# Transposes of the second phase made by DMA on SyncE's queue instead of TensorE, with the steps moved

## The reference, cut to what matters

```python
xn = rmsnorm(x, norm_attn_g)
q, k, v, gate_b, gate_c, h = split(xn @ w_in)      # three groups of 4 heads x 64; windows 128, 512, 2048, dilations 1, 4, 16
attn = heads' softmax attention per group, groups weighted by their softmax denominators
conv = gate_b * causal_conv3(gate_c * h)
x = x + concat(attn, conv) @ w_out
x = x + square(relu(rmsnorm(x, norm_mlp_g) @ w_up)) @ w_down
y = rmsnorm(x, norm_final_g)
```

## Time and profile before

| | us |
|---|---|
| median of 3 runs | 3246.47 (3242.42 to 3248.24) |
| the profiled execution, its own time | 3248.41 |
| its span, slowest core | 3246.7 |
| spans of the eight cores | 3194.0 to 3246.7 |
| TensorE busy in the span | 3035.3 (93%) |
| VectorE, ScalarE, GpSimd busy | 1334.1, 1080.6, 187.3 |

### The profile page before, as it was taken

The page is one execution under the profiler, slowest core; times in us unless marked ns, Lnnn a source line. Parts: engine busy times, 40 slices in busy tenths (PEclk is TensorE's granted clock), DMA queues, the critical chain, the costliest instruction groups (busy, mean ns, idle before and its releaser), DMA issues.

```text
span 3246.7 us, 65561 instructions; the slowest of 8 cores (3194.0 to 3246.7 us)
## 1 busy us (share of the span) xinstructions
PE 3035.3 (93%) x23299; PEld 1948.8 (60%) x23299; DVE 1334.1 (41%) x2927; ACT 1080.6 (33%) x2399; POOL 187.3 (6%) x232
## 2 busy tenths in 40 slices
PE   5997859899997799999999999999999999999998
PEld 2654435565554466666666666666666666666665
DVE  5355426637444234333343333333343333433332
ACT  4244225436334223222232323323232233323232
POOL 3101200101000000000000000000000000000000
PEclk9998979999998899999999999999999999999999
DMA  9124925536134825444254343543535425333130
GB/s 198 37 67 115 79 43 130 129 70 149 34 131 178 206 51 132 104 103 120 55 141 109 86 119 58 155 109 69 122 64 145 121 57 125 77 117 107 38 114 21
DMA packets 168411, 331.62 MB, mean 102 GB/s; under 512 B 31840, under 2 KB 124000, under 8 KB 165984
## 3 DMA queue, kind: packets, MB, share of 16 engines
q1 hardware_dynamic: 94080, 172.92, 16.5%
q0 software_dynamic: 70672, 67.19, 15.9%
q10 hardware_dynamic: 3344, 87.30, 9.2%
HBM read 309.57 MB, written 176.39 MB: 150 GB/s over the span
## 4 chain that ended last, share of the span: by engine, by line
PE 84%; DMA 4%; ACT 3%; issue 3%; DVE 3%; SPq 1%; another core or an unknown queue 1%; POOL 0%; ACTq 0%; DVEq 0%; POOLq 0%
PE pp L750 28%; PE pp L739 26%; PE pp L566 12%; PE pp L678 7%; PE pp L533 4%; DMA NZ<-osb 3%; ACT junkB L875 1%; PE pp L536 1%; PE pp L688 1%; DMA w_in_sb<-w_in 1%; PE pp L582 1%; SPq L1328 1%; PE pp L701 1%; PE pp L663 1%; PE pp L511 1%
## 5 line engine op out<-in xcount | busy, mean ns | idle before, releaser
L739 PE MATMUL pp<-xn1T,w_up_sb 128*128 128x256 bf16 (+1 forms) x8448 | 1071.2, 271 | 29.3 <-ACT hr L901 26.6
L750 PE MATMUL pp<-w_down_sb,h1T 128*128 128x512 bf16 x4160 | 1057.9, 379 | 17.9 <-DMA w_down_sb<-w_down_b 17.9
L739 PEld LDWEIGHTS pp<-xn1T,w_up_sb 128*128 128x128 bf16 x8448 | 804.1, 98 | 281.1 <-issue 39.3
L901 ACT ACTIVATE hr<-pp 128x256 bf16<-128x256 f32 (+1 forms) x1056 | 394.6, 380 | 1181.6 <-PE pp L739 1173.9
L1150 DVE TENSOR_TENSOR h1T<-hr 128x256 bf16<-128x256 bf16 (+1 forms) x1056 | 301.0, 289 | 1003.1 <-ACT hr L901 936.5
L750 PEld LDWEIGHTS pp<-w_down_sb,h1T 128*128 128x128 bf16 x4160 | 402.7, 98 | 299.6 <-issue 19.0
L566 PE MATMUL pp<-xnT,w_in_sb 128*128 128x512 bf16 x2304 | 536.6, 382 | 24.2 <-DMA w_in_sb<-w_in 8.8
L566 PEld LDWEIGHTS pp<-xnT,w_in_sb 128*128 128x128 bf16 x2304 | 212.0, 98 | 268.9 <-issue 37.2
L678 PE MATMUL pp<-w_out_sb,attnT 128*128 128x512 bf16 x1040 | 249.7, 384 | 9.0 <-DMA attnT<-cvT 9.0
L858 ACT ACTIVATE PT<-pp 128x1024 bf16<-128x1024 f32 x171 | 174.2, 1023 | 145.3 <-PE pp L586 143.8
L1022 DVE TENSOR_TENSOR PT<-PT,mask 128x1024 bf16<-128x1024 bf16 (+1 forms) x192 | 129.4, 674 | 198.8 <-ACT PT L858 185.3
(11 more groups left out here) (136 smaller groups left out, 1984.0 us busy)
## 6 DMA issues: line engine op xcount, KB each, us to landing
kvs<-ck ACTq DMA_DIRECT2D x16, 4080.0 KB, 21.2
xt<-xp SPq DMA_DIRECT2D x64, 512.0 KB, 5.3
xtB<-xp SPq DMA_DIRECT2D x64, 512.0 KB, 3.8
yp<-xtB SPq DMA_DIRECT2D x64, 512.0 KB, 3.1
NZ<-osb SPq DMA_DIRECT2D x192, 130.0 KB, 2.3
NZt<-NZ SPq DMA_DIRECT2D x64, 390.0 KB, 4.6
kvs<-ck ACTq DMA_DIRECT2D x16, 1008.0 KB, 6.4
sK<-ck POOLq DMA_DIRECT2D x52, 256.0 KB, 6.7
```

The source lines that it names most:

```text
L739: ins = e.matmul(bank(v % 2)[:, 0:N], lhsT=w_up_sb[:, i // 8, kc, (i % 8) * 128:(i % 8 + 1) * 128], rhs=xn1T[T % 2][:, kc, 0:N], start=kc ...
L750: ins = e.matmul(psD[s][:, half * 512:(half + 1) * 512], lhsT=h1T[v % NH][:, s * 128:(s + 1) * 128], rhs=w_down_sb[:, i, half * 512:(half ...
L901: e.activation(out=hr[v % NHR][:, 0:N], in_=bank(v % 2)[:, 0:N], func=AF.Relu).then_inc(s_hr, 1)
```

## The change

The steps b and sT, and the first half of d, leave TensorE; the copies after b (ScalarE) and sT (VectorE) go. In their place SyncE issues DMA transposes from SBUF to SBUF: b from attn_n to attnT, a new step t from xn1 to xn1T, and sT from sK to sKTc. What d keeps is VectorE's multiply by the gain, in place in xn1T. Who waited for TensorE's transposes now waits for these DMAs (a, n and d on VectorE, c and sS on TensorE, the load of sK on GpSimd's queue). The bank B_T is not used any more. In FIRST_B and SLOTS the steps stand elsewhere: b two slots earlier, in the slots of a; c in 13, 15, 17 and 19 (was 15, 17, 19, 21); n in 19 and 23 (was 21 and 25); t in 20 and 24; d in 26 and 30 (was 25 and 29); sT in 13 and 25 (was 17 and 31).

```diff
 FIRST_B = [(-1, "LX", 0, 0), (-1, "LX", 0, 1), (-1, "LN", 0, 0), (0, "LN", 0, 1), (0, "LC", 0, 0), (0, "a", 0, 0),
-           (2, "b", 0, 0), (2, "LN", 1, 0), (3, "a", 0, 1), (4, "c", 0, 0, 0), (5, "b", 0, 1), (5, "LN", 1, 1),
-           (6, "c", 0, 0, 1), (8, "c", 0, 1, 0), (9, "n", 0, 0), (10, "c", 0, 1, 1), (11, "d", 0, 0), (13, "n", 0, 1),
-           (14, "d", 0, 1)]
+           (1, "b", 0, 0), (2, "LN", 1, 0), (3, "a", 0, 1), (4, "b", 0, 1), (5, "c", 0, 0, 0), (5, "LN", 1, 1),
+           (6, "c", 0, 0, 1), (8, "c", 0, 1, 0), (9, "n", 0, 0), (9, "t", 0, 0), (10, "c", 0, 1, 1), (12, "d", 0, 0),
+           (13, "n", 0, 1), (13, "t", 0, 1), (15, "d", 0, 1)]
...
-        SLOTS = {1: [("sP", -1, 0), ("LC", 1), ("E", -1, 0)], 3: [("E", -1, 1)], 5: [("y", -1, 0), ("ST", -1, 0), ("LX", 1, 0), ("a", 1, 0)],
-                 7: [("y", -1, 1), ("ST", -1, 1), ("LX", 1, 1), ("b", 1, 0)], 9: [("a", 1, 1)], 11: [("b", 1, 1), ("LN", 2, 0)],
-                 13: [("LN", 2, 1)], 15: [("c", 1, 0, 0)], 17: [("c", 1, 0, 1), ("sT", -1, 1)], 19: [("c", 1, 1, 0)],
-                 21: [("n", 1, 0), ("c", 1, 1, 1)], 23: [("sS", -1, 1)], 25: [("d", 1, 0), ("n", 1, 1)], 26: [("sP", -1, 1)],
-                 29: [("d", 1, 1)], 31: [("sT", 0, 0)], 33: [("sS", 0, 0)]}
+
+        SLOTS = {1: [("sP", -1, 0), ("LC", 1), ("E", -1, 0)], 3: [("E", -1, 1)],
+                 5: [("y", -1, 0), ("ST", -1, 0), ("LX", 1, 0), ("a", 1, 0), ("b", 1, 0)],
+                 7: [("y", -1, 1), ("ST", -1, 1), ("LX", 1, 1)], 9: [("a", 1, 1), ("b", 1, 1)], 11: [("LN", 2, 0)],
+                 13: [("LN", 2, 1), ("c", 1, 0, 0), ("sT", -1, 1)], 15: [("c", 1, 0, 1)], 17: [("c", 1, 1, 0)],
+                 19: [("n", 1, 0), ("c", 1, 1, 1)], 20: [("t", 1, 0)], 23: [("sS", -1, 1), ("n", 1, 1)], 24: [("t", 1, 1)],
+                 25: [("sT", 0, 0)], 26: [("sP", -1, 1), ("d", 1, 0)], 30: [("d", 1, 1)], 33: [("sS", 0, 0)]}
...
         def b_bank(T):
 
-            return (0, 1) if T == 0 else (B_T, B_M)
+            return 1 if T == 0 else B_M
+
+        def tr_done(W, sems, q):
+
+            W.wait_ge(sems[q % 2], 16 * (q // 2 + 1))
...
             for kind, T, i, *half in events:
-                pst = bank_bf(b_bank(T)[0] if kind in "bd" else B_T).rearrange("p (k t) -> p k t", k=8)
-                if kind == "b":
+                if kind == "c":
                     q = nsubs_before(T) + i
+                    W.wait_ge(s_wo, 16)
                     if T == 0:
                         W.wait_ge(s_free["act"], P.nev["act"])
                         W.wait_ge(s_free["dve"], P.nev["dve"])
-                    W.wait_ge(s_an, q + 1)
-                    W.wait_ge(s_xn1T, nsubs_before(T))
-                    W.wait_ge(s_aTs, q)
-                    W.wait_ge(s_ktc, min(2 * T - 3, NBAT))
-                    for kc in range(6):
-                        ins = e.transpose(out=pst[:, kc, :], in_=attn_n[:, kc * 128:(kc + 1) * 128], identity=ident[:])
-                    ins.then_inc(s_aT, 1)
-                elif kind == "c":
-                    q = nsubs_before(T) + i
-                    W.wait_ge(s_wo, 16)
                     if T < 32:
-                        W.wait_ge(s_aTs, q + 1)
+                        tr_done(W, s_aT, q)
                     else:
                         W.wait_ge(s_sat, 1)
                     W.wait_ge(s_bcv[q % 2], 16 * (q // 2 + 1))
@@ -675,35 +670,13 @@
                         W.wait_ge(s_x1, m)
                     W.wait_ge(s_so, min(2 * T - 3, NBAT))
                     for kc in range(8):
-                        ins = e.matmul(bank(b_bank(T)[1]), lhsT=attnT[q % 2][:, kc, :],
+                        ins = e.matmul(bank(b_bank(T)), lhsT=attnT[q % 2][:, kc, :],
                                        rhs=w_out_sb[:, kc, half[0] * 512:(half[0] + 1) * 512], start=kc == 0, stop=kc == 7)
                     ins.then_inc(s_m, 1)
-                elif kind == "d":
-                    q = nsubs_before(T) + i
-                    W.wait_ge(s_xn1, q + 1)
-                    W.wait_ge(s_aTs, min(nsubs_before(T) + nsub(T), 64))
-                    W.wait_ge(s_ktc, min(2 * T - 2, NBAT))
-                    W.wait_ge(s_xn1T, q)
-                    for kc in range(8):
-                        ins = e.transpose(out=pst[:, kc, :], in_=xn1[:, kc * 128:(kc + 1) * 128], identity=ident[:])
-                    ins.then_inc(s_xT1, 1)
-                elif kind == "sT":
-
-                    b = T
-                    g, bb, t0, nq = BATCHES[b]
-                    W.wait_ge(s_ldk, 16 * (b + 1))
-                    if b % 2 == 0:
-                        W.wait_ge(s_xn1T, nsubs_before(b // 2 + 1) + nsub(b // 2 + 1))
-                    else:
-                        W.wait_ge(s_aTs, nsubs_before(b // 2 + 2) + 2)
-                    for u in range(4):
-                        for p in range(2):
-                            ins = e.transpose(out=pst[:, u * 2 + p, :], in_=sK[:, u, p * 128:(p + 1) * 128], identity=ident[:])
-                    ins.then_inc(s_kt, 1)
                 elif kind == "sS":
                     b = T
                     g, bb, t0, nq = BATCHES[b]
-                    W.wait_ge(s_ktc, b + 1)
+                    W.wait_ge(s_kt, 16 * (b + 1))
                     W.wait_ge(s_x1, done_x1(b // 2 + 1 + b % 2))
                     if b:
...
-                if kind == "b":
-                    q = nsubs_before(T) + i
-                    W.wait_ge(s_aT, q + 1)
-                    if q >= 2:
-                        W.wait_ge(s_m, 2 * (q - 1))
-                    e.activation(out=attnT[q % 2][:, 0:6, :], in_=pst[:, 0:6, :], func=AF.Copy).then_inc(s_aTs, 1)
-                elif kind == "c" and half[0] == 1:
+                if kind == "c" and half[0] == 1:
...
                 elif kind == "a":
                     q = nsubs_before(T) + i
                     if T:
-                        W.wait_ge(s_xT1, nsubs_before(T))
+                        tr_done(W, s_xT1, 2 * T - 2)
+                        tr_done(W, s_xT1, 2 * T - 1)
                     else:
                         phase_a_left(W)
                     nzv = NZt[q % 2][:].rearrange("p (g h e) -> p g h e", g=3, h=4)
                     W.wait_ge(s_bnz[q % 2], 16 * (q // 2 + 1))
                     if q:
-                        W.wait_ge(s_aT, q)
+                        tr_done(W, s_aT, q - 1)
...
-                elif kind == "sT":
-                    b = T
-                    W.wait_ge(s_kt, b + 1)
-                    if b:
-                        W.wait_ge(s_ss, b)
-                    e.tensor_copy(out=sKTc[:].rearrange("p u k t -> p (u k) t"), in_=pst).then_inc(s_ktc, 1)
...
                 elif kind == "n":
                     q = nsubs_before(T) + i
                     xrow = xtB[sl][:, i, :]
                     W.wait_ge(s_br, q + 1)
                     W.wait_ge(s_x1, 2 * q + 2)
-                    W.wait_ge(s_xT1, q)
+                    if q:
+                        tr_done(W, s_xT1, q - 1)
                     e.tensor_scalar(out=xn1[:], in0=xrow, scalar1=rsB[NORM["c", T, i] % 4], scalar2=None,
                                     op0=ALU.mult).then_inc(s_xn1, 1)
                 elif kind == "d":
                     q = nsubs_before(T) + i
-                    W.wait_ge(s_xT1, q + 1)
+                    xr = xn1T[sl][:, :, i * 128:(i + 1) * 128]
+                    tr_done(W, s_xT1, q)
                     W.wait_ge(s_ldgm, 16)
-                    if T >= 2:
-                        W.wait_ge(s_u, 32 * (T - 1))
-                    e.tensor_tensor(out=xn1T[sl][:, :, i * 128:(i + 1) * 128], in0=pst,
+                    e.tensor_tensor(out=xr, in0=xr,
                                     in1=g_mlp_sb[:, :].unsqueeze(2).broadcast_to([128, 8, 128]), op=ALU.mult
                                     ).then_inc(s_xn1T, 1)
                 elif kind == "up":
...
                 if b:
-                    W.wait_ge(s_kt, b)
+                    W.wait_ge(s_kt, 16 * b)
...
+                elif kind == "b":
+                    q = nsubs_before(T) + i
+                    W.wait_ge(s_an, q + 1)
+                    if q >= 2:
+                        W.wait_ge(s_m, 2 * (q - 1))
+                    e.dma_start_transpose(out=attnT[q % 2][:, 0:6, :], in_=attn_n).then_inc(s_aT[q % 2], 16)
+                elif kind == "t":
+                    q = nsubs_before(T) + i
+                    W.wait_ge(s_xn1, q + 1)
+                    if T >= 2:
+                        W.wait_ge(s_u, 32 * (T - 1))
+                    e.dma_start_transpose(out=xn1T[sl][:, :, i * 128:(i + 1) * 128], in_=xn1[:]).then_inc(s_xT1[q % 2], 16)
+                elif kind == "sT":
+                    b = T
+                    W.wait_ge(s_ldk, 16 * (b + 1))
+                    if b:
+                        W.wait_ge(s_ss, b)
+                    e.dma_start_transpose(out=sKTc[:].rearrange("p u k t -> p (u k) t"),
```

(22 more changed lines are left out.)

## The result

The changed kernel takes **3537.2 us** (median of 4 runs, 3516.0 to 3544.9) against 3246.6 us of the kernel before (4 runs, 3242.4 to 3248.2). The ratio is 1.088, its 95% interval 1.082 to 1.094. The change costs 291 us; the forecast was a gain of 62, and the result lies 227 us above the top of the range.

A forecast was written before the change was run, and what follows sets the result against it. TensorE, busy 93% of the span, was taken to bound the kernel. -72 us removed and +10 at the first phase's end made -62: 3248.4 to 3186.4 us profiled, median 1.9 lower, 3184.5; range 3168 to 3310.

The forecast's parts named there:

- What is removed, -72: TensorE's transposes of attention rows, cached keys and MLP rows: 74.5 us, less 2.3 ahead of the wait for w_down.
- ScalarE's squares at the tile's edge: Named as what TensorE waits for once per tile in the second phase: 26.6 us over 33 tiles.
- The landing, 4 us: Time for a DMA transpose on SP's queue to land, bounded from other DMAs; 2.5 to 3.5 us at plain pace.
- upper bound of 20 to 26 us: Transpose landing beside the cache copy: 64 KB took 6.0 us more there, and transposes have three or four times the rows.
- The deadlines: Time each second-phase transpose is allowed before its user waits, from 9.0 us for b(T+1,0); none missed at 4 us, cost 0.
- its cover: Slack between a second-phase transpose's issue and its user, first of all 9.0 us; 25 us for sT(T-1,1).
- The end of the first phase, +10: First attention-row transposes meet the weight loads: 3 to 7 us for the first, 2 to 5 for three others; bounds 0 to 25.
- sum of -62: Whole kernel: -72 for transposes removed and +10 at the first phase's end, giving 3184.5 us; forecast chance 0.52.
- Rival B: Even tiles: the cache copy slows some transposes, 16 tiles x 2.5 = +40 us, kernel at 3226; chance 0.12.
- Rival A: Transposes are long, so SP's queue or TensorE at c waits; 3284 us at 1.35 us per block; chance 0.29.
- r = 0.92: Time in us per 128x128 block from which b(T+1,0) passes its allowed 9.0 us at c in slot 13.
- 0.29 for slower: Chance that the whole kernel gets slower, all of it from long transposes; 0.12 of it below 3310 us.

The follow-up runs named there:

- run 3: Changed kernel with the same cache copies issued after up 28 instead of up 13, half the bytes in each tile; 3170.8 us, 0.980 of the kernel before.
- run 4: Kernel before the change, with its cache copies moved in the same way (after up 28, half in each tile); 3223.4 us, ratio 0.996.
- run 1: Changed kernel without the DRAM to DRAM copies of the caches; 3168.4 us, 0.979 of the kernel before.

## Why the prediction was wrong

- **What is removed, -72.** Nearly right. In runs 3 and 4 the second phase, first up to last up, takes 2082 to 2089 us against 2151 to 2152 (2080 to 2085 against 2150 to 2152 without the copy): core by core -63 to -71, on average -66 with the copy and -69 without. The few us that are missing fit the per-tile pace, 64.5 measured for 64.2. What the forecast calls ScalarE's squares at the tile's edge are its relus.
- **The landing, 4 us.** Right where no copy is in flight: medians of 3.2 to 4.7 in runs 1 and 3. The upper bound of 20 to 26 us was an error. It scaled the 6.0 us that 64 KB of attnT had lost beside the copy with the number of rows, and so held the copy at 22.1 us whatever stood beside it. It took 70.0, and landings went to 74.8.
- **The deadlines.** The list was right (9.0, 13, 25, 13 us), and all are met in tiles without a copy, but for 3 us at c beside the weight loads. In the copy's tiles sT, which had the longest allowance of all, is missed first, because it is issued within some 1.5 us of the copy. What I called its cover, slack of 25 us, was not enough to ask for; the question was what else is in flight when it is issued.
- **The end of the first phase, +10.** Right in kind, too small. The first up of run 3 comes at 1061.6 against 1041.3 in run 4 (+20, mean of eight cores), on the slowest core 1074.0 against 1052.5 (+21.5); inside my bounds of 0 to 25. b(0,0) landed after 20.0 us where I had added 3 to 7.
- **The forecast as a whole.** The sum of -62 is near what the change does without the meeting: -56 without the copy, -53 with it moved. That 3170.8 and 3172.7 us lie 12 to 14 below the forecast of 3184.5 is no merit of the sum: moving the copy also gives back some 13 us of w_down's wait, which the forecast did not count.
- **Rival B was the cause, and its price the failed step.** Place and mechanism were the forecast's: even tiles, sT done when the copy ends, t after it. It priced this at 2.5 us in each of 16 tiles, +40 over the forecast. (Its 3226 is 1.5 us more than that sum gives.) It cost 291 + 62 = 353 over it, 22 us a tile, with single stalls of 50 us. The clock may have added to this: in the stretch with the stall it was 0.67 of full, and the changed kernel's second phase is 378 to 384 us longer than the 2082 to 2089 of run 3, of which the waits name 349. B's bounds were missing: it had one price, from a 64 KB transfer, for transfers three and four times as large, in packets of 250 bytes beside some of 65,280, and it took the copy's own 22.1 us as fixed.
- **Rival A**, on which the whole chance of "slower" stood, was wrong in mechanism. 256 KB land in a median of 3.2 us, the issue included, so a block of 128x128 takes 0.4 us; r = 0.92 was needed. The Trainium skill's 1309 ns a block (VectorE: DVE Perf Modes, The three transpose paths), taken one block after another, does not describe this transfer: by an estimate from that figure eight blocks would be 10.5 us, and the measured 3.2 decides. 0.29 for slower came from there and not from B; B had chances for a gain only.

## What to carry to other kernels

Before work is moved onto the DMA engines, list what is in flight on them at the moment of each new issue, not only how busy they are on average: a transpose in 256-byte packets issued beside a bulk DRAM copy landed up to 18 times later than alone (58.6 for 3.2 us, 74.8 for 4.2) and made the copy up to three times longer, and the cure was to issue the copy behind the tile's last transpose (3537 to 3171 us, with no byte fewer). When the trace shows a small transfer slowed beside a large one, bound both of them from above, the large one too; a bound that scales only the small one has no ceiling in it. Cutting a copy into small pieces and issuing them all at once moved the cost to the engine that issues it.

## What the hardware showed beyond that

- Transpose and copy slow each other: the copy of 4080 KB 22.1 to 70.0 us, the transposes from 3 to 5 us to as much as 58.6 and 74.8, while the engines are 96% busy at 80 GB/s, most of it in the transposes' packets. Without the key transposes the copy's median is back at 21.5. The worst meetings are those in which the transpose goes out 0.5 to 1.8 us ahead of the copy's large part.
- Instruction fetches suffer too, it seems. A fetch (q8) took 0.4% of sixteen engines over 64 us for four packets, 1.0 us each, in the tile without a copy from 1653 to 1717. From 1725 to 1745 one took 7.8%, 25 us, and TensorE then stood 14.72 us in the middle of a group of c, put down to "issue". It went on 1.9 us after that fetch ended. The fetches before the other two pieces of that kind (19.8 and 26.6 us) took only 1.2 and 1.1 us once they ran, but TensorE went on 1.4 and 1.5 us after they ended, and it is so in all six such pieces over 5 us on the eight cores after 1000 us (1.3 to 1.9 us), with the fetch before that one 44 us or more back. That fits a fetch held up in a queue; no run tests it.

```profile
q8 instruction: 1, 0.02, 7.8%
```

- An engine can stand at the issue of a DMA. Three issues of long rows take 1.77 us; six of 1 KB pieces 13.60, most of it at the sixth, while the same bytes in 14 issues over 14 ups mostly take 0.8 each. SP stood 40.04 us at one issue of a transpose while the DMA engines were held up, and 10 to 43 us at eight issues of t; 1.2 us in the median.
- A copy that nobody waits for cost the kernel before as well: 0.4% come from moving it, and the wait that goes is the one in tile 0, where w_down still loads at up 13.
